# Four-layer hybrid backbone: softmax rows scaled through a diagonal matrix on GpSimd, and four reorderings in the hyena and window layers

## What is computed

```python
s = einsum('bqkgd,bskd->bkgqs', q, k) * scale
p = softmax(s, axis=-1)                      # layer C: with a sink column, dropped after
o = einsum('bkgqs,bskd->bqkgd', p, v)
h = h + m[2] * rmsnorm(o @ w_out (+ b_out), g[1])
f = conv_ffn(modulate(rmsnorm(h, g[2]), m[3], m[4]))
h = h + m[5] * rmsnorm(f, g[3])
```

## Time and profile before

| | |
|---|---|
| median of 3 runs | 2288.19 us |
| the profiled execution's own time | 2291.39 us |
| its span, first to last instruction | 2289.6 us |
| mean granted TensorE clock | 0.979 |
| attention of layer 0, about | 170 to 227 us |
| long convolution, about | 824 to 922 us |
| input of layer C, about | 1345 to 1418 us |
| attention of layer C, about | 1418 to 1509 us |
| attention of the last layer, about | 2007 to 2051 us |

### The profile page before, as it was taken

How to read it: one execution, slowest core, us unless ns; L and a number is a source line. 1 busy time by engine, 2 the same in 40 slices (tenths; PEclk the granted TensorE clock), 3 DMA queues, 4 the chain that set the end, 5 groups by cost and what they waited for, 6 DMA issues and landing times.

```text
span 2289.6 us, 28755 instructions
## 1 busy us (share of the span) xinstructions
PE 2175.4 (95%) x11688; PEld 1767.1 (77%) x11688; DVE 1437.8 (63%) x2212; ACT 884.0 (39%) x1329; POOL 217.5 (9%) x253
## 2 busy tenths in 40 slices
PE   5999999999999988899999999999999999998998
PEld 3877888888787756788888787478888878868996
DVE  2426558887756532667887754866787776655553
ACT  3327443332244311443332243854333223455543
POOL 0000011110010014111110001100111100100110
PEclk7999999999999999999999999999999999999999
DMA  9460335546532210334546532022454563214554
GB/s 308 141 209 19 111 101 161 171 150 217 194 126 83 83 37 19 102 100 158 166 149 220 202 103 65 1 84 82 149 165 156 184 211 120 99 45 131 185 182 140
DMA packets 224745, 304.98 MB, mean 133 GB/s; under 512 B 6738, under 2 KB 153243, under 8 KB 224486
## 3 DMA queue, kind: packets, MB, share of 16 engines
q1 hardware_dynamic: 220541, 290.11, 39.0%
q0 software_dynamic: 3664, 12.87, 1.7%
q10 hardware_dynamic: 409, 0.16, 0.0%
HBM read 302.00 MB, written 1.11 MB: 132 GB/s over the span
## 4 chain that ended last, share of the span: by engine, by line
PE 78%; DVE 10%; ACT 5%; DMA 3%; issue 2%; SPq 1%; POOL 1%; ACTq 0%; DVEq 0%; POOLq 0%
PE lo L639 16%; PE lo L640 16%; PE lo L641 16%; PE lo L705 4%; PE lo L706 4%; PE lo L707 4%; DVE w_lo L1383 2%; ACT w_hi L1059 2%; PE lo L973 2%; PE hi L705 2%; PE hi L707 2%; PE hi L706 2%; DMA w_raw<-in_ffn_w_down 1%; PE hi L986 1%; PE stat L705 1%
## 5 line engine op out<-in xcount | busy, mean ns | idle before, releaser
L639 PE MATMUL lo<-u_hi,w_hi 128*128 128x512 f32 (+1 forms) x2072 | 736.5, 355 | 9.0 <-DVE w_lo L1383 3.8
L640 PE MATMUL lo<-u_lo,w_hi 128*128 128x512 f32 (+1 forms) x2072 | 723.2, 349 | 0.0
L641 PE MATMUL lo<-u_hi,w_lo 128*128 128x512 f32 (+1 forms) x2072 | 722.6, 349 | 0.0
L1383 DVE TENSOR_TENSOR w_lo<-w_raw,w_hi 128x2048 fp32r<-128x2048 f32 (+1 forms) x182 | 406.7, 2235 | 356.9 <-ACT w_hi L1059 355.7
L1059 ACT ACTIVATE w_hi<-w_raw 128x2048 fp32r<-128x2048 f32 (+1 forms) x182 | 339.5, 1867 | 478.9 <-DMA w_raw<-in_ffn_w_down 266.7
L639 PEld LDWEIGHTS lo<-u_hi,w_hi 128*128 128x128 f32 x2072 | 394.7, 191 | 74.1 <-issue 19.3
L641 PEld LDWEIGHTS lo<-u_hi,w_lo 128*128 128x128 f32 x2072 | 394.5, 190 | 50.1
L640 PEld LDWEIGHTS lo<-u_lo,w_hi 128*128 128x128 f32 x2072 | 394.7, 190 | 49.7 <-issue 1.2
L1400 DVE SCALAR_TENSOR_TENSOR mod_acc<-mod_raw,silu_c,mod_acc 128x512 f32<-128x512 f32 x504 | 394.6, 848 | 9.9 <-DMA mod_raw<-in_mod_w 9.9
L1912 POOL TENSOR_TENSOR mid_lo<-conv,mid_hi 128x512 fp32r<-128x512 f32 (+1 forms) x88 | 117.8, 1359 | 1055.7 <-ACT mid_hi L1362 1055.7
L705 PE MATMUL lo<-w_hi,mid_hi 128*128 128x512 f32 x374 | 147.4, 394 | 3.7 <-DVE u_raw L1450 2.6
(11 more groups left out here) (296 smaller groups left out, 2698.2 us busy)
## 6 DMA issues: line engine op xcount, KB each, us to landing
w_raw<-in_ffn_w_up SPq DMA_DIRECT2D x88, 1024.0 KB, 5.1
mod_raw<-in_mod_w SPq DMA_DIRECT2D x144, 512.0 KB, 4.0
w_raw<-in_ffn_w_down SPq DMA_DIRECT2D x40, 1024.0 KB, 5.1
mod_unit<-in_mod_w SPq DMA_DIRECT2D x24, 1024.0 KB, 6.8
w_raw<-in_a_w_qkv SPq DMA_DIRECT2D x12, 1024.0 KB, 5.2
w_raw<-in_b_w_in SPq DMA_DIRECT2D x12, 1024.0 KB, 5.1
w_raw<-in_a_w_out SPq DMA_DIRECT2D x8, 1024.0 KB, 5.1
w_raw<-in_ffn_w_down SPq DMA_DIRECT2D x8, 512.0 KB, 3.6
```

What stands on the lines that cost most here:

```text
L639: mm(o, h3[:, k, c], x, start=(first and k == 0), stop=False)
L640: mm(o, h3[:, k, c], y, start=False, stop=False)
L641: ins = mm(o, l3[:, k, c], x, start=False, stop=(last and k == nr - 1))
L1383: tt(WL[:, n % 3, 0:words], RAW[:, n % 3, 0:words], WH[:, n % 3, 0:words].bitcast(F32), ALU.subtract).then_inc(lo_ready, 1)
```

## The change

Five edits. (1) In attention, VectorE writes only the reciprocal of the row sums; GpSimd multiplies the identity by it into `inv_sum` (128 x 128 per block of queries, eight buffers where `squares` lies), and TensorE multiplies the unscaled probabilities by this diagonal matrix instead of transposing scaled ones. GpSimd loads bias and gates after its last diagonal. (2) In the hyena, `fill` is gone: the first output tile comes after `inverse(3)`. (3) In layer C the key tile moves from second to third, and its turn behind those of chunks 0 to 3. (4) ScalarE takes one square root of a constant after the square sums of the first column half of every sub-layer. (5) In sub-layers with a bias, VectorE's `lo(L + 1)` moves from b = 0 to after the diagonal of b = 1.

```diff
-        TILES += [("c_w_qkv", _j, 0, KT, 0, TW), ("c_w_qkv", _j, 0, KT, D, P)]
-        TILES += [("c_w_qkv", _j, 0, KT, TW * t, TW) for t in range(1, 4)]
+        TILES += [("c_w_qkv", _j, 0, KT, TW * t, TW) for t in range(2)]
+        TILES += [("c_w_qkv", _j, 0, KT, D, P)]
+        TILES += [("c_w_qkv", _j, 0, KT, TW * t, TW) for t in range(2, 4)]
...
-      2: [[0, 1], [8], [2, 3], [4, 5], [6, 7], [9]],
+      2: [[0, 1], [2, 3], [8], [4, 5], [6, 7], [9]],
...
-TURNS = {..., 2: [8, 9, 0, 1, 2, 3, 4, 5, 6, 7], ...}
+TURNS = {..., 2: [0, 1, 2, 3, 8, 9, 4, 5, 6, 7], ...}
...
-           2: {2: {0: [0], 2: [1], 4: [2], 6: [3]}, 3: {2: [4], 5: [5]}, ...
+           2: {2: {0: [0], 4: [1]}, 3: {0: [2], 2: [3], 4: [4], 6: [5]}, ...
...
+        RD = place("inv_sum", [P, 8, P], at=SQ_AT)
...
     # TensorE, turn(x); ND[i][x] counts the diagonals ahead of item x
-                            last = nc.tensor.transpose(t_bank(i, x)[:, at * P:(at + 1) * P], p[:, src:src + P], ident)
+                            last = mm(t_bank(i, x)[:, at * P:(at + 1) * P], p[:, src:src + P], RD[:, (ND[i][x] + b) % 8, :],
+                                      start=True, stop=True)
...
     # TensorE, long_conv
                     if w < 3:
                         forward(w + 1)
-                    else:
-                        fill()
                     inverse(w)
...
-                    long_conv(lambda: x_tiles(2, UH, UL, arrive, free, [0]))
+                    long_conv()
...
-                x_tiles(2 * i, UH, UL, arrive, free, range(KIND[i] == 1, 2), end=True)
+                x_phase(2 * i, UH, UL, arrive, free)
...
     # ScalarE, x_phase
                 for b in range(NB):
                     o_square(k, 0, b)
+                f(R1[:, 1, 4:5], eps[:, :], ACT.Sqrt)
...
     # VectorE, x_phase
                     residual(k, b)
-                    if b == 0:
+                    if b == 0 and not has_bias(k):
                         lo(L + 1)
...
                     if more and not (b == 1 and NB == 2):
                         diagonal(k + 1, b)
+                    if b == 1 and has_bias(k):
+                        lo(L + 1)
...
     # VectorE, normalise
-                    link(nc.vector.reciprocal(sl[:, 3, 0:nb], sl[:, 2, 0:nb]))
-                    for b in range(nb):
-                        c0 = b * (CTX if A else CTX + 4)
-                        s = slice(c0, c0 + TOK // nb)
-                        ins = ts(p[:, s], p[:, s], sl[:, 3, b:b + 1], None, ALU.mult)
-                    ins.then_inc(s_norm, 1)
+                    nc.vector.reciprocal(sl[:, 3, 0:nb], sl[:, 2, 0:nb]).then_inc(s_inv, 1)
...
     # GpSimd
+                def diagonals(x):
+                    h, t = HALVES[i][x]
+                    sl = small[:, x % 6, :, :]
+                    pool.wait_ge(s_inv, G + x + 1)
+                    free = [y for y in range(x) if ND[i][y] <= ND[i][x + 1] - 9]
+                    if free:
+                        pool.wait_ge(p_turned, G + free[-1] + 1)
+                    for b in range(1 if t < 2 else 2):
+                        ins = nc.gpsimd.tensor_scalar(RD[:, (ND[i][x] + b) % 8, :], ident, sl[:, 3, b:b + 1], None, ALU.mult)
+                    ins.then_inc(s_norm, 1)
+
+                for x in range(-4, NH[i]):
+                    if KIND[i] == 2 and x + 4 < NH[i]:
+                        sink(x + 4)
+                    if x >= 0:
+                        diagonals(x)
...
                     attention_in(i)
+                    attention(i)
                     if KIND[i] == 2:
-                        sinks(i)
-                        pool.wait_ge(s_ready, ahead(NH, i) + NH[i])
                         load_bias(i)
                     pool.wait_ge(gr_rows, i + 1)
-                    pool.wait_ge(q_roped, turns_ahead(i) + 10)
```

More of the change, by code:

```diff
@@ L85 @@
 CH = {0: [[8, 9], [0, 1], [2, 3], [4, 5], [6, 7], [10, 11]],
-      2: [[0, 1], [8], [2, 3], [4, 5], [6, 7], [9]],
+      2: [[0, 1], [2, 3], [8], [4, 5], [6, 7], [9]],
       3: [[0, 1], [8, 9], [2, 3], [4, 5], [6, 7], [10, 11]]}
-TURNS = {0: [8, 9, 0, 1, 2, 3, 4, 5, 6, 7], 2: [8, 9, 0, 1, 2, 3, 4, 5, 6, 7], 3: [0, 1, 8, 9, 2, 3, 4, 5, 6, 7]}
+TURNS = {0: [8, 9, 0, 1, 2, 3, 4, 5, 6, 7], 2: [0, 1, 2, 3, 8, 9, 4, 5, 6, 7], 3: [0, 1, 8, 9, 2, 3, 4, 5, 6, 7]}
 TURN_AT = {0: {2: {0: [0], 3: [1]}, 3: {0: [2], 2: [3], 4: [4], 6: [5]}, 4: {2: [6], 5: [7]}, 5: {1: [8], 3: [9]}},
-           2: {2: {0: [0], 2: [1], 4: [2], 6: [3]}, 3: {2: [4], 5: [5]}, 4: {2: [6], 5: [7]}, 5: {1: [8], 3: [9]}},
+           2: {2: {0: [0], 4: [1]}, 3: {0: [2], 2: [3], 4: [4], 6: [5]}, 4: {2: [6], 5: [7]}, 5: {1: [8], 3: [9]}},
            3: {2: {0: [0], 2: [1], 5: [2]}, 3: {2: [3], 4: [4], 6: [5]}, 4: {2: [6], 5: [7]}, 5: {1: [8], 3: [9]}}}
@@ L226, in build @@
         SB = place("sum_o_base", [P, 4])
-        R1 = place("inv_o", [P, 2, 4])
+        R1 = place("inv_o", [P, 2, 5])
         HSUM = place("sum_h", [P, 4])
@@ L319, in build @@
         v_turned, v_ready = sem("v_turned"), sem("v_ready")
-        s_ready, s_max, s_exp, s_norm, sink_set = (sem("s_ready"), sem("s_max"), sem("s_exp"), sem("s_norm"),
-                                                   sem("sink_set"))
+        s_ready, s_max, s_exp, s_inv, s_norm, sink_set = (sem("s_ready"), sem("s_max"), sem("s_exp"), sem("s_inv"),
+                                                          sem("s_norm"), sem("sink_set"))
         p_turned, p_evac, pv_done, ao_hi, ao_lo = (sem("p_turned"), sem("p_evac"), sem("pv_done"), sem("ao_hi"),
@@ L345, in build @@
         NH = {i: len(HALVES[i]) for i in ATT}
+        ND = {i: [sum(1 if t < 2 else 2 for h, t in HALVES[i][:x]) for x in range(NH[i] + 1)] for i in ATT}
         GROUPS = {i: HEADS[i] // STEP[i] for i in ATT}
@@ L695, in u_turns, with x_phase @@
                     last.then_inc(u_turned, 1)
-            def x_tiles(k, X, Y, arrive, free, ts, end=False):
+            def x_phase(k, X, Y, arrive, free):
                 n0, nt, NB = XFIRST[k], XTILES[k], XN[k]
@@ L719, in finished @@
                         ins.then_inc(x_done, 1)
-                for t in ts:
+                for t in range(2 * nt - 2):
                     n, (h, tt) = n0 + t, divmod(t, nt)
@@ L752, in x_tiles @@
                 n = n0 + 2 * nt - 2
-                for b in range(NB if end else 0):
+                for b in range(NB):
                     if nt == 2:
@@ L948, in filter_stage, with long_conv @@
                         last.then_inc(f_spec, 1)
-            def long_conv(fill):
+            def long_conv():
                 def turn(w):
@@ L1044, in _ @@
                     tile(n0 + t, q0 + t, N, UH, UL, True, True)
-                x_tiles(2 * i + 1, MH, ML, lambda k, b=i * FM: pe.wait_ge(ml_ready, b + k + 1),
-                        lambda b, q=q0 + FM: (released(q - 2 + b // 2),), range(10), end=True)
+                x_phase(2 * i + 1, MH, ML, lambda k, b=i * FM: pe.wait_ge(ml_ready, b + k + 1),
+                        lambda b, q=q0 + FM: (released(q - 2 + b // 2),))
         @block.scalar
@@ L1613, in normalise @@
                     nb = 1 if t < 2 else 2
-                    sl, p = small[:, x % 6, :, :], PB[:, x % 6, :]
+                    sl = small[:, x % 6, :, :]
                     dve.wait_ge(s_exp, G + x + 1)
-                    link(nc.vector.reciprocal(sl[:, 3, 0:nb], sl[:, 2, 0:nb]))
-                    for b in range(nb):
-                        c0 = b * (CTX if A else CTX + 4)
-                        s = slice(c0, c0 + TOK // nb)
-                        ins = ts(p[:, s], p[:, s], sl[:, 3, b:b + 1], None, ALU.mult)
-                    ins.then_inc(s_norm, 1)
+                    nc.vector.reciprocal(sl[:, 3, 0:nb], sl[:, 2, 0:nb]).then_inc(s_inv, 1)
                 def step(x):
@@ L1824, in attention_in, with attention, sink @@
                         tt(QK[:, r, 0:SEQ], QK[:, r, 0:SEQ], cosT, ALU.mult).then_inc(q_cos, 1)
-            def sinks(i):
+            def attention(i):
                 G = ahead(NH, i)
-                for x, (h, t) in enumerate(HALVES[i]):
+                def sink(x):
+                    h, t = HALVES[i][x]
                     if x >= 6:
@@ L1947, in QCOS @@
 def QCOS(i, j):
-    return sum(10 if KIND[k] == 0 else 8 for k in range(i) if KIND[k] != 1) + (j if KIND[i] == 0 else j - 2)
+    return (sum(10 if KIND[k] == 0 else 8 for k in range(i) if KIND[k] != 1)
+            + sum(KIND[i] == 0 or r < 8 for r in TURNS[i][:j]))
 _INS = ["x", "c", "ctx", "c_ctx", "mod_w", "mod_b", "norm_g", "ffn_w_up", "ffn_conv_w", "ffn_conv_b", "ffn_w_down",
```

## The result

The change makes the kernel slower: 2308.04 us (median of 4 runs, 2307.85 to 2309.28) against 2289.24 us for the kernel before on the same chip, ratio 1.0084 with a 95% interval of 1.0067 to 1.0102, or +19.2 us. The forecast of 2278 us was on the wrong side, and its range ended at 2286.

What follows compares the result with a forecast made beforehand. TensorE, busy 95% of the span, was taken as the bound. Edits 2 to 5 and -1.0 for edit 1 summed to -10.1 us: 2281.3 from the profiled 2291.39, 2278 us on the median, range 2267 to 2286.

Steps and rivals of the forecast that it cites:

- the last term of edit 1: Attention turns on TensorE: transpose 287 ns, matmul with a diagonal 290 ns, 352 of them, +0.5 us.
- Its factor of four for FP32: Attention turns: by this rule each of 352 would take over 1 us, costing far over 100 us; the forecast rejected it.
- D: GpSimd's time to write one diagonal in attention, taken as 0.40 us, with 0.19 and 0.73 kept as limits.
- 32 D - 12.5: Layer C attention steps: microseconds the wait for GpSimd's diagonals adds, from 16 steps with one and 8 with two.
- -1.8 for the freed VectorE: First seven steps of layer C and last items of each attention: freed VectorE time gains 1.8 us.
- The rival with D above 0.72: Layer C attention: slow GpSimd diagonals make the whole change slower; 2297 us at D = 1.0; chance 6%.
- -6.2 forecast: Edit 2, hyena: gap -4.2, low clock -2.6, possible new low clock +0.6; edit 3, layer C input: gap -3.5, low clock -2.7.
- the +0.6: Hyena, edit 2: allowance in us for a lowered clock behind the new 2.1 us wait ahead of inverse(3).
- "Nothing" for the later load of the fourth output tile: Hyena output projection: tile loaded 9.1 us later, ready at 927.1, wanted by TensorE at 931.5, so no cost.
- -0.6 for it alone: End of the last mixer: moving the square root's table load off the chain to the 5.51 us gap gains 0.6 us.
- The low clock that I priced at +3.4: Ends of both biased mixers: TensorE idles about 4.3 us in one piece, then half clock costs 1.7 us, twice.
- my -9.1 for edits 2 to 5: Terms outside attention, in us: -4.2 - 2.6 + 0.6 - 3.5 - 2.7 - 0.6 + 0.5 + 3.4.

Runs made afterwards that it cites:

- Experiments 4 and 5: 4: edit 1 on the kernel before, VectorE writing the diagonals instead of GpSimd, 2310.75 us; 5: the kernel before with every turning transpose issued twice, 2310.01 us.
- experiment 3: Edit 1 alone on the kernel before, with its diagonals and waits, but TensorE transposing with the identity, rows left unscaled: 2295.33 us, ratio 1.0027.

## Why the prediction was wrong

**The step that failed** is the last term of edit 1: "transpose 287 ns, matmul with a diagonal, as in `u_turns`, 290; 352 of them, +0.5". It should have been about +21. Experiments 4 and 5 measured +20.8 and +20.4. (352 times the 3 ns between the two means is 1.1 us, not 0.5, but that is not what failed.) Both durations were read rightly, and both are the time of one row in a pipelined engine. What I did not do is count rows: the code of `u_turns` makes 2 matmuls for each column chunk, so 4 for a tile of two chunks, and the trace of before lists 8 rows for it; the transposes of four blocks are 4 rows. A float32 matmul stood in the trace as two instructions all along. Start to start, the kernel before had the price too: 0.11 us for a block turned by transpose, and twice as much for one in `u_turns`, where 8 rows, 4 blocks, take 1551.71 - 1550.82 = 0.89 us:

```profile
1550.82 1.06 PE L693 MATMUL hi<-conv,h 128*128 128x128 f32 x8
1551.71 1.06 PE L693 MATMUL lo<-conv,h 128*128 128x128 f32 x8
```

From the same wrong reading I dismissed a rule of the Trainium skill. Its factor of four for FP32 (the Trainium skill, TensorE: Matmul & The Clock Gate, Terms) was used as a time on each row, "the 287 and 290 ns speak against it". They don't: the direction was right. The size in this kernel is two, 0.89 us for four blocks against 0.44, and the time is 21 us and not over 100, because what doubles is the 0.11 us from start to start and not the 0.29 of a row, and because a part of it fills idle time. The Trainium skill (FP8 and Floating Point Precision, TensorE Precision Notes) puts a true FP32 product at four passes through the array. A product with fp32r weights (the type of `w_hi` and `w_lo`) starts every 0.227 us for 512 columns (917.39 to 917.62 in the kernel after), which is 0.057 for 128, and a block turned by the diagonal takes 0.22. The ratio is 3.9, which agrees if a product of the fp32r kind is one pass; no run here counts passes.

**Edit 1's diagonals.** D was 0.602 where I took 0.40. The form of the term held: 32 D - 12.5 gives +6.8 at 0.60, with -1.8 for the freed VectorE +5.0, and experiment 3 measured +6.2 (3.9 to 8.7). With this D alone put right, the forecast would still have been -3.6 us, inside its range; it is the turns' +21 that brings it to about +17. The rival with D above 0.72 was on the right side for the wrong reason.

**Edit 2** was right: -6.2 forecast, -6.6 measured. The new wait is 1.84 us for 2.1 forecast, and no low clock follows it, so the +0.6 was not needed. "Nothing" for the later load of the fourth output tile held in every kernel with edit 2 and without edit 1 (4.9 to 5.1 us to landing) and failed by 2.4 us in the whole change. There the load took 9.0 us where I had put 5.1, and I had asked only when TensorE wants the tile, and not what stands behind its `lo` on VectorE.

**Edit 3** was right in kind: -6.2 forecast, -7.6 measured (-10.5 to -4.6), gap and low clock both gone. The matmuls are not the same in number, as I wrote, but the same in columns.

**Edit 4.** I had folded its effect on the biased mixers into edit 5 and counted -0.6 for it alone, in the last mixer; by the traces it takes 1.27 us off each biased mixer's first gap and 0.6 off the last mixer's.

**Edit 5.** The chain that I followed is there: with edits 2 to 5 the first gap in layer C is 0.32 us for 0.4 forecast, and the second gap comes later. But TensorE's idle time does not collect in one piece of 4.3 us: it is 1.43 us inside `u_turns` and 2.6 us behind. The low clock that I priced at +3.4 came behind one of the two mixers in the trace of edits 2 to 5 (the one of layer B, clock 0.51 for 3.4 us behind a gap of 2.65), and cost half of that. These 1.7 us, the 0.6 of edit 2 and the 1.4 by which edit 3 gave more are 3.7 of the 4.2 us between my -9.1 for edits 2 to 5 and the measured -13.3. The interval of that (-16.2 to -10.5) is too wide to check such a sum closely.

## What to carry to other kernels

Before a cheap-looking instruction is swapped for another, count its rows in the trace against the calls in the code, and price it start to start where the engine runs without a wait; the mean duration of a pipelined row hides a doubling. On an engine that is busy 95% of the span, work that is moved onto it from an engine with slack is a loss until shown otherwise. And try the parts of a change alone: here one part took back more than four others gave, and among those four one is probably better left out.

## What the runs showed of the hardware

A matmul with float32 operands appears as two matmul and two weight-load instructions (704 of each for 352 blocks), each 0.11 us start to start for 128 columns; a transpose of the same block is one, also 0.11 us.

Multiplying a 128 x 128 float32 tile by a scalar per partition takes GpSimd 0.602 us, steadily (0.599 to 0.605 over 112), and VectorE 0.286.

The length of a gap alone does not say whether TensorE's clock falls behind it. The kernel with edits 2, 3 and 4 resumed in layer C after a wait of 2.09 us at half clock, 1.2 GHz; timeline and window:

```profile
1552.97 2.08 PE L694 MATMUL stat<-conv,h 128*128 128x128 f32 x8 [2.09 <-DVE conv L1470]
```

```profile
1553.00:1556.40 3.40, 3.40 (x16) 3.40 (x17) 2.17 (x1) 2.22 (x3) 0.00 (x0) 0.51 0.00 0
```

The kernel after had a longer wait in the same place and stayed at the full 2.4 GHz, in the same two views:

```profile
1584.75 1.16 PE L696 MATMUL stat<-conv,h 128*128 128x128 f32 x8 [2.62 <-DVE conv L1473]
```

```profile
1582.00:1590.00 8.00, 4.62 (x39) 4.34 (x38) 5.11 (x10) 6.09 (x10) 0.00 (x0) 1.00 0.00 0
```

Even two executions of the same kernel differ. Behind the mixer of layer B the kernel after waited 2.61 us in one and 2.63 us in the other; timeline and window, first the one and then the repeat:

```profile
977.47 1.16 PE L696 MATMUL stat<-conv,h 128*128 128x128 f32 x8 [2.61 <-DVE conv L1473]
...
976.73 1.25 PE L696 MATMUL stat<-conv,h 128*128 128x128 f32 x8 [2.63 <-DVE conv L1473]
```

```profile
977.50:980.90 3.40, 2.91 (x24) 2.72 (x24) 2.17 (x1) 3.37 (x6) 0.00 (x0) 1.00 0.00 0
...
976.80:980.20 3.40, 3.40 (x20) 3.40 (x21) 2.21 (x1) 2.66 (x5) 0.00 (x0) 0.63 0.00 0
```

The granted clock is 1.00 behind the first and 0.63 on average behind the second. Such a term should be priced as a chance, not as a sum.
